# A two-layer decoder trunk on one core: the first norm's root carried by two columns, and query squares summed by a four-column selector

## What is computed

```
def rms_norm(x, w):
    xf = x.astype(jnp.float32)
    y = xf * lax.rsqrt(jnp.mean(xf * xf, axis=-1, keepdims=True) + EPS)
    return (y * w.astype(jnp.float32)).astype(x.dtype)
...
    for i in range(DEPTH):
        m, j = i % N_MIXERS, i // N_MIXERS
        h = rms_norm(x, mix_norm[i])
...
    q = rms_norm(q.reshape(bsz, seq, G, HG, DH), q_norm)
```

## Time and profile before

| | us |
|---|---|
| median of 3 runs | 2619.43 (2617.18 to 2620.1) |
| the profiled execution | 2623.78 |
| its span, first to last instruction | 2622.1 |
| PE busy | 2607.7 (99% of the span) |
| DVE busy | 1798.3 (69%) |
| ACT busy | 1428.6 (54%) |
| POOL busy | 222.7 (8%) |
| mean granted TensorE clock | 0.996 of full speed |

### The profile page before, as it was taken

The page is one execution under the profiler, slowest core; times in us unless marked ns, Lnnn a source line. Parts: engine busy times, 40 slices in busy tenths (PEclk is TensorE's granted clock), DMA queues, the critical chain, the costliest instruction groups (busy, mean ns, idle before and its releaser), DMA issues. The chain is left out here.

```text
span 2622.1 us, 46276 instructions
## 1 busy us (share of the span) xinstructions
PE 2607.7 (99%) x15345; PEld 2293.1 (87%) x15345; DVE 1798.3 (69%) x2606; ACT 1428.6 (54%) x2210; POOL 222.7 (8%) x198
## 2 busy tenths in 40 slices
PE   9999999999999999999999999999999999999999
PEld 8888888888888888888888888888888888888888
DVE  8677777775677777776555766666777777775444
ACT  6667767654455555554444555655555555554443
POOL 0121112222100000000111001001300000000000
PEclk9999999999999999999999999999999999999999
DMA  5655555655555556556666565323555555556665
GB/s 207 210 199 195 194 189 198 195 174 190 188 188 189 191 187 191 187 189 186 191 189 197 180 225 190 99 92 101 185 191 187 189 189 188 188 188 191 188 188 170
DMA packets 137452, 482.04 MB, mean 184 GB/s; under 512 B 15248, under 2 KB 17296, under 8 KB 136352
## 3 DMA queue, kind: packets, MB, share of 16 engines
q1 hardware_dynamic: 134528, 467.72, 56.1%
q0 software_dynamic: 2336, 12.65, 1.4%
q10 hardware_dynamic: 512, 0.65, 0.1%
HBM read 478.80 MB, written 2.16 MB: 183 GB/s over the span
## 5 line engine op out<-in xcount | busy, mean ns | idle before, releaser
L765 PE MATMUL ps<-xn,w_hi 128*128 128x512 f32 x4768 | 1665.1, 393 | 0.0
L1092 DVE TENSOR_TENSOR w_lo<-raw,w_hi 128x1024 fp32r<-128x1024 f32 x900 | 1102.7, 1228 | 669.7 <-ACT w_hi L409 668.6
L409 ACT ACTIVATE w_hi<-raw 128x1024 fp32r<-128x1024 f32 x900 | 937.9, 1044 | 841.6 <-PE ps L765 819.1
L764 PE MATMUL ps<-xn,w_lo 128*128 128x256 f32 x4768 | 1347.3, 283 | 3.0 <-DVE xn L1118 1.5
L765 PEld LDWEIGHTS ps<-xn,w_hi 128*128 128x128 f32 x4768 | 894.7, 188 | 199.1 <-issue 1.7
L764 PEld LDWEIGHTS ps<-xn,w_lo 128*128 128x128 f32 x4768 | 903.2, 189 | 9.3 <-issue 3.1
L765 PE MATMUL ps<-hid,w_hi 128*128 128x512 f32 x1408 | 488.2, 391 | 0.0
L764 PE MATMUL ps<-hid,w_lo 128*128 128x256 f32 x1408 | 394.3, 280 | 0.0
L765 PEld LDWEIGHTS ps<-hid,w_hi 128*128 128x128 f32 x1408 | 263.3, 187 | 57.7
L764 PEld LDWEIGHTS ps<-hid,w_lo 128*128 128x128 f32 x1408 | 266.1, 189 | 0.0
L765 PE MATMUL ps<-y_ssm,w_hi 128*128 128x512 f32 x512 | 178.2, 392 | 0.0
(11 more groups left out here) (240 smaller groups left out, 1739.8 us busy)
## 6 DMA issues: line engine op xcount, KB each, us to landing
raw<-w_gu SPq DMA_DIRECT2D x352, 512.0 KB, 4.0
raw<-w_ssm_in SPq DMA_DIRECT2D x162, 512.0 KB, 3.7
raw<-w_down SPq DMA_DIRECT2D x128, 448.0 KB, 3.4
raw<-w_nsa_in SPq DMA_DIRECT2D x82, 512.0 KB, 3.9
raw<-w_ssm_out SPq DMA_DIRECT2D x64, 512.0 KB, 4.3
raw<-w_down SPq DMA_DIRECT2D x64, 512.0 KB, 3.6
raw<-w_nsa_out SPq DMA_DIRECT2D x32, 512.0 KB, 3.7
wcum<-cum_scratch POOLq DMA_DIRECT2D x8, 1024.0 KB, 7.6
```

What stands on the lines that cost most here:

```text
L409: act.activation(w_hi[:, slot, 0:n * P], raw[:, slot, 0:n * P], ACT.Copy).then_inc(unit_rounded, 1)
L764: pe.matmul(acc[:, n:2 * n], w_lo[:, slot, cols], x[:, kb, 0:n], start=(kb == 0), stop=False, skip_group_check=True)
L765: mm = pe.matmul(acc[:, 0:2 * n], w_hi[:, slot, cols], x[:, kb, 0:2 * n], start=False, stop=(kb == p.blocks - 1), skip_group_check=True)
L1092: TT(w_lo[:, slot, 0:n * P], raw[:, slot, 0:n * P], w_hi[:, slot, 0:n * P].bitcast(F32), ALU.subtract).then_inc(unit_split, 1)
```

## The change

Three edits.

First, the first norm. The sums are taken with 64 columns of ones instead of 128 (the output stands on 64 partitions). ACT takes the root of one partition alone, 1x256. PE turns these 256 values to two columns of 128 (two matmuls of one row and one column), DVE takes the reciprocal of 128x2, multiplies the identity by each column (two diagonal matrices side by side in `psq`), and PE multiplies ones by them, which spreads the reciprocal root over all partitions in `ps[5]`. `scaled` reads it there. ACT rounds weight unit 1, and DVE splits it, behind this and no longer ahead of it. PE does 16 matmuls on ones behind it instead of 32.

Second, the query squares. A held selector `sel[:, h]` of four columns, whose column h is ones, adds up head h's squares into row h of a 4x256 output: four matmuls of 256 columns. ACT copies the four rows to `gate[64:68]`, and two matmuls turn them to columns (`query_turn`).

Third, their place: `query_sums` stands ahead of head 0's scores, and `query_turn` behind them.

```
-            for w in range(2):
-                round_unit(w, unit_sizes[w])
-            stream_std(0)
-            for w in range(2, RING):
+            round_unit(0, unit_sizes[0])
+            act.wait_ge(ssum_done, 1)
+            act.activation(rstd[0:1], ps[2][0:1, 0:T], ACT.Sqrt, scale=1.0 / (D_TILES * P), bias=eps[0:1, 0:1]).then_inc(std_ready, 1)
+            for w in range(1, RING):
                 round_unit(w, unit_sizes[w])
...
                 if v == 0:
                     act.wait_ge(qss_done, G + 1)
+                    act.activation(qrow, ps[6][0:HPG, 0:T], ACT.Copy).then_inc(qrow_ready, 1)
+                    act.wait_ge(qss_turned, G + 1)
                     act.wait_ge(exp_done, HPG * G)
...
-                    mm = pe.matmul(ps[2][:, 0:T], ones[:], xsq[c][:, m], start=(c + m == 0), stop=(c + m == 6))
+                    mm = pe.matmul(ps[2][0:HD, 0:T], ones[:, 0:HD], xsq[c][:, m], start=(c + m == 0), stop=(c + m == 6))
             mm.then_inc(ssum_done, 1)
-            for m in range(2 * WARM):
+            pe.wait_ge(std_ready, 1)
+            for c in range(2):
+                mm = pe.matmul(ps[4][:, c:c + 1], rstd[0:1, c * L:(c + 1) * L], ones[0:1, 0:1], start=True, stop=True)
+            mm.then_inc(std_turned, 1)
+            pe.wait_ge(diag_ready, 2)
+            pe.matmul(ps[5][:, 0:T], ones[:], psq[:], start=True, stop=True).then_inc(rstd_spread, 1)
+            for m in range(WARM):
                 pe.matmul(ps[3][:, 0:P], ones[:], ones[:], start=True, stop=True)
...
                 pe.wait_ge(pt0_ready, HPG * G)
+                pe.wait_ge(sel_set, 1)
                 for h in range(HPG):
-                    for c in range(2):
-                        a = c * HPG + h
-                        mm = pe.matmul(ps[6][:, a:a + 1], qsq[:, h, c * L:(c + 1) * L], ones[:, 0:1], start=True, stop=True)
+                    mm = pe.matmul(ps[6][0:HPG, 0:T], sel[:, h], qsq[:, h], start=(h == 0), stop=(h == HPG - 1))
                 mm.then_inc(qss_done, 1)
+
+            def query_turn(G):
+
+                pe.wait_ge(qrow_ready, G + 1)
+                for c in range(2):
+                    mm = pe.matmul(ps[6][:, c * HPG:(c + 1) * HPG], qrow[:, c * L:(c + 1) * L], ident[64:64 + HPG, 64:64 + HPG], start=True, stop=True)
+                mm.then_inc(qss_turned, 1)
...
+                if v == 0:
+                    query_sums(G)
                 if v < 4:
                     scores(G, v)
                 if v == 0:
-                    query_sums(G)
+                    query_turn(G)
...
-                TT(xy[k][:], xg[k][:], rstd[:].unsqueeze(1).broadcast_to([P, 4, T]), ALU.mult).then_inc(xy_ready, 1)
+                TT(xy[k][:], xg[k][:], ps[5][:, 0:T].unsqueeze(1).broadcast_to([P, 4, T]), ALU.mult).then_inc(xy_ready, 1)
...
-            for w in range(2):
-                split_unit(w, unit_sizes[w])
-            stream_rstd(0)
+            split_unit(0, unit_sizes[0])
+            dve.wait_ge(std_turned, 1)
+            dve.reciprocal(rc[:], ps[4][:, 0:2]).then_inc(rstd_ready, 1)
+            dve.wait_ge(rstd_ready, 1)
+            dve.wait_ge(ident_set, 1)
+            for c in range(2):
+                TS(psq[:, c * L:(c + 1) * L], ident[:], rc[:, c:c + 1], None, ALU.mult).then_inc(diag_ready, 1)
+            split_unit(1, unit_sizes[1])
             dve.wait_ge(xg_ready, 4)
+            dve.wait_ge(rstd_spread, 1)
```

More of the change, by code:

```diff
@@ L179, in trunk @@
         psq = sb("psq", [P, T])
+        rc = sb("rc", [P, 2])
+        sel = sb("sel", [P, HPG, HPG])
         def col(name, i=0):
@@ L228, in trunk @@
             rq = sb("rq", [P, 2, HPG], F32, st)
+            qrow = gate[64:64 + HPG]
             kqn = sb("kqn", [P, 1], F32, st)
@@ L272, in trunk @@
         ones_set, ident_set, eps_set = sem("ones_set"), sem("ident_set"), sem("eps_set")
-        ident_zero = sem("ident_zero")
+        ident_zero, sel_zero, sel_set = sem("ident_zero"), sem("sel_zero"), sem("sel_set")
+        std_turned, diag_ready, rstd_spread = sem("std_turned"), sem("diag_ready"), sem("rstd_spread")
         resid_step = sem("resid_step")
@@ L307, in trunk @@
         qsq_ready, qss_done, qstd_ready, rq_step = sem("qsq_ready"), sem("qss_done"), sem("qstd_ready"), sem("rq_step")
+        qrow_ready, qss_turned = sem("qrow_ready"), sem("qss_turned")
         floor_set, mask_zero, mask_ready = sem("floor_set"), sem("mask_zero"), sem("mask_ready")
@@ L1520, in _ @@
             pool.memset(ident[:], 0.0).then_inc(ident_zero, 1)
+            pool.memset(sel[:], 0.0).then_inc(sel_zero, 1)
             pool.wait_ge(ident_zero, 1)
@@ L1540, in stream_squares @@
                 loop(pool, 1, D_TILES, add)
+            pool.wait_ge(sel_zero, 1)
+            pool.memset(sel[:].rearrange("p a b -> p (a b)")[:, 0:HPG * HPG:HPG + 1], 1.0).then_inc(sel_set, 1)
             pool.wait_ge(consts_landed, 32)
```

## The result

| | before | after |
|---|---|---|
| median, us | 2619.43 (2617.18 to 2620.1) | 2630.4 (2629.04 to 2632.9) |
| ratio, 95% interval | | 1.0046 [1.0033, 1.0059] |
| the profiled execution, us | 2623.78 | 2631.52 |
| its span, us | 2622.1 | 2629.8 |
| mean granted clock | 0.996 | 0.998 |

The account below looks back on a forecast made before the run. PE, busy 99% of the span, was taken to bound the kernel; 0.9 + 3.6 + 3.2 - 3.4 = +4.3 us on the median of 2619.4 gave 2623.7 us, range 2617.5 to 2628.

Parts of the forecast that it names:

- The clock, -3.4: Behind the query sums: two stretches of 3.4 us at half speed are given back, 1.7 us each, -3.4 us.
- rival 1: Clock not given back, as new gaps make it fall: +6.0 us with one stretch, +7.7 with two; chance 0.27.
- The sums of the first norm, 0: First norm's sums with 64 held columns: pace goes by streamed columns, 32 passes take 6.9 us as before, no change.
- Rival 2: Few held columns stream faster, half the time a pass with 64: -1.5 us in all, 2617.9; chance 0.12.
- The chain, +0.9: Root, turn, reciprocal, diagonals and weight split behind the first norm's sums: first product at 17.1, not 16.19, +0.9 us.
- The query sums and the turn, +0.9 a group: Query step: sums by selector +0.1 us, turning four rows to columns +0.75; 0.9 a group, 3.6 in four.
- The waits, +3.2: PE waits for POOL's last square before the scores: 1.4 us in the first group, 2.0 in the last; +3.2 us.

Follow-up runs that it names:

- e1: The kernel before with an unused array of 96 bytes where the change has its own arrays: 2624.86 us, 1.0022 against the kernel before.
- e6: The kernel before with an unused array of 256 bytes in the place of the change's arrays: 2618.18 us, 0.9991 against the kernel before.
- e5: The change with an unused array of 160 bytes behind `sel`, shifting what follows by 256 bytes in all: 2626.05 us, 1.0022 against the kernel before.
- e2: The change with an unused array of 32 bytes behind `sel`, shifting what follows by 128 bytes in all: 2633.8 us, 1.0057 against the kernel before.
- e9: The kernel before with only the two weight arrays moved by 128 bytes, against all streamed arrays: 2642.52 us, 1.0085 against the kernel before.
- e10: The change's second and third edits alone (query sums, turn, their place), arrays behind shifted by 256 bytes: 2626.46 us, 1.0025 against the kernel before.
- e8: The change's first edit alone (the first norm), arrays behind shifted by 256 bytes: 2619.88 us, 1.0 against the kernel before.
- e12: e11 with the 16 single-column matmuls of the key sums also spread over one unit, two behind each pair: 2618.32 us, 0.9992 against the kernel before.
- e11: The kernel before with each group's eight single-column query-sum matmuls spread over the next weight unit, one per pair: 2619.93 us, 0.9997 against the kernel before.

## Why the prediction was wrong, step by step

**The failed step is a term that the sum puts at nothing without a reason: it costs each edit where it runs, and takes the two new arrays (`rc`, `sel`) as free.** With them the three activation arrays behind stand 96 bytes further from the weights, and their matmuls run slower. These 96 bytes cost 6.0 us in the traces (e1 against e6) and 1.0022 [1.0012, 1.0032] in the timed runs, more than half of the change's 11 us. The rows from which it could have been foreseen don't exist in the trace of before, where all streamed and held arrays start at the same place modulo 256. But that the arrays behind would move could be read off the diff, and it wanted a term with bounds. Without this cost the change stays inside the range (e5, +5.6); with it, the time lies above the range. On speed by place the Trainium skill has, on the page "SBUF — State Buffer", section "Specifications (TRN2)", lines of 16 bytes, with a penalty for crossing to a new one. All shifts here are multiples of 16, so that rule gives no change, and the counts of e1, e2 and e9 say otherwise; the measurement decides.

**The clock, -3.4: mis-sized, it is about 0 in the timed runs.** They put the queries at 6.5 (e10), and the four steps take 6.3 without any gain of the clock. In the traces the two stretches behind the query sums did go. But I took the change of the median to be that of the one profiled execution, whose clock of 0.996 lay at the low end: the 27 timed executions of before beside e10 have a mean of 0.9977, from 0.996 to 0.999, and the eleven of e10 have 0.9977 too. There was less to be given back: e6, which has the work of before, loses one query stretch in its trace, and its span is 6.3 us shorter than that of before. And rival 1's mechanism takes some of it back. In two of five traces with the new queries (e2 and e5) the last group's sums, behind their idle time, run at half speed; those of e5 take 3.50 in place of 1.89:

```profile
1768.98 3.50 PE L1004 MATMUL ps<-q,sel 128*4 128x256 f32 x8 [1.94 <-POOL q L1643]
```

At a place that costs nothing the change is +5.6 (e5), which lies between my +4.3 and the +6.0 of rival 1 with one stretch, nearer to the rival; the interval of 3.4 to 8.1 holds both. So the steps and waits of my forecast were right, and its term for the clock was not: there rival 1, with its 0.27, had the better case, and stood on the right row, the gap of 2.0 us.

**The sums of the first norm, 0: right.** 7.12 against 7.07. Rival 2, that few held columns are faster, falls: 64 and 4 held columns both stream 256 in 0.216.

**The chain, +0.9: 0.66.** The first product comes 10.06 behind the first sum where the forecast has 17.1 - 6.79 = 10.3. The root was 0.47, the turn 0.60 and the reciprocal 0.17, as bounded; the diagonals overlap, 0.40 to the split. In the timed runs the norm alone is at 1.0 (e8), within 0.1%.

**The query sums and the turn, +0.9 a group: 0.84.** The step is 0.75 longer, and 0.09 goes to entering the sums: 3.4 in four groups, forecast 3.6. The turn is 0.53 where I had 0.75.

**The waits, +3.2: 2.9**, at the two places named and none at the other two. The 3.2 of PE's idle time (1.25 and 1.94) is no like measure, since in the last group PE waited some 0.2 before the change too, which the forecast had taken off; the steps of e10 are 6.3 longer in all, and 3.4 of it is the step's own work. Together 6.3, forecast 6.8; the spans of e10 and e6 give 6.8, and the timed runs 1.0025 [1.0016, 1.0034], which is 6.5.

**The sum again.** From the trace of before to that of the change: +6.8 for the queries, +1.7 at the start (0.66 of it the chain), +6.0 for the place; the half-speed time falls from 20.4 us to 6.8 outside the start, -6.8. That is +7.7, and the spans differ by 2629.8 - 2622.1 = 7.7; that it closes to the tenth is luck, since each term is good to about 0.5. Timed, the parts are 1.0022 (e1), 1.0025 (e10) and 1.0 (e8), 1.0047 together, and the change has 1.0046. At a place that costs nothing it has 1.0022 (e5), +5.6 us, where the forecast had +4.3.

## What to carry to other kernels

When an edit adds an array, ask what stands behind it: a held and a streamed operand whose starts agree modulo 256 bytes ran fastest here, so round what is added up to 256 bytes, or put it last. When a matmul phase in which nothing was changed gets slower while PE is busy for the whole of it, count instructions in equal windows. And before a clock loss is put into a sum, look at the granted clock of several executions, since a profiled one need not be the median's.

## What the runs showed of the hardware

- The pace of a pair of passes (256 and 512 streamed columns, 128 held, a load of weights ahead of each) depends on the distance of the two operands' starts modulo 256: 346.0 ns at 0, 349.3 at 96, 350.6 at 128, whichever of the two was moved; moving both by 128 changes nothing. Other distances weren't tried, nor which part of the pass is longer, and one trace (e12) is slow on `y_ssm` at a distance of 0. Over all 6944 pairs of e9 4.5 ns would be 31 us, and it lost 22. The loss isn't even: from 700 to 1180 us the passes fall by 1.3% (2770 to 2735), from 40 to 540 us by 0.4% (3087 to 3075). Why, was not followed up.
- The clock can fall behind single-column matmuls though the profile counts PE as busy in them: 1.9 us of them in a row were followed by 3.4 us at 1.2 GHz in one or two groups of four, and the same matmuls woven between pairs by none (e11, e12). It differs from execution to execution of one kernel, 0.996 to 0.999 in the mean clock and 2615 to 2624 us in the time.
- Going from weights of 128 held columns to the selector's four takes 0.09 us more, and going from the selector to the scores another 0.09. The page "TensorEngine Tiling (Array Packing)" of the Trainium skill, section "Tiling Modes", has it that a change of tiling mode drains the engine. The trace doesn't show whether these are changes of mode, so it neither bears the rule out nor speaks against it; a load of the held block that isn't hidden could cost the same.
